# The first two weight chunks piece by piece over both halves of x, in a two-block fp32 decoder kernel

## What is computed

```python
def rmsnorm(x, g):
    xf = x.astype(jnp.float32)
    y = xf * lax.rsqrt(jnp.mean(xf * xf, axis=-1, keepdims=True) + NORM_EPS)
    return (y * g.astype(jnp.float32)).astype(x.dtype)

def split_proj(h, w_in, n_kv):
    proj = h @ w_in          # (256 x 1024) @ (1024 x 2304)
    ...
```

## Time and profile before

| | us |
|---|---|
| median of 3 runs (873.58 to 873.85) | 873.74 |
| the profiled execution | 873.88 |
| its span, first to last instruction | 872.1 |
| TensorE matmuls busy | 861.9 (99%) |
| VectorE busy | 562.4 (64%) |
| ScalarE busy | 509.8 (58%) |
| GpSimd busy | 121.9 (14%) |

### The profile page before, as it was taken

One profiled execution on the slowest core, in us unless ns is written; L12 is line 12 of the kernel. 1 busy time (PEld: TensorE's weight loads), 2 busy tenths in 40 slices (PEclk: granted clock), 3 DMA queues, 4 the chain that ended last, 5 costly groups with the idle time before them and its releaser, 6 DMA issues.

```text
span 872.1 us, 12071 instructions
## 1 busy us (share of the span) xinstructions
PE 861.9 (99%) x4426; PEld 702.8 (81%) x4426; DVE 562.4 (64%) x991; ACT 509.8 (58%) x907; POOL 121.9 (14%) x99
## 2 busy tenths in 40 slices
PE   8999999999999999999999999999999999999996
PEld 5877888778888878888888888888878888888885
DVE  6966866677766777755555446576778655555444
ACT  6668466765886864644444334777865644444332
POOL 0122053110153500000000000153510000000000
PEclk9999999999999999999999999999999999999999
DMA  8823563445533336655555555444345655555531
GB/s 307 281 65 105 187 201 135 147 145 173 175 129 131 129 114 209 209 182 179 187 193 194 193 192 172 151 140 145 99 144 187 211 184 192 193 191 175 194 117 48
DMA packets 94765, 146.15 MB, mean 168 GB/s; under 512 B 6516, under 2 KB 54900, under 8 KB 94708
## 3 DMA queue, kind: packets, MB, share of 16 engines
q1 hardware_dynamic: 92820, 139.52, 48.0%
q0 software_dynamic: 1296, 4.72, 1.5%
q10 hardware_dynamic: 592, 1.15, 0.4%
HBM read 144.32 MB, written 1.05 MB: 167 GB/s over the span
## 4 chain that ended last, share of the span: by engine, by line
PE 93%; DVE 2%; ACT 2%; issue 1%; DMA 1%; SPq 0%; POOLq 0%; POOL 0%; ACTq 0%; DVEq 0%
PE bank L1166 79%; PE bank L1114 7%; PE bank L1317 1%; PE bank L1243 1%; PE bank L1221 1%; PE bank L1218 1%; ACT hyb_E L1559 1%; DMA raw<-in_w_in_a 1%; PE bank L1246 1%; ACT hi L1337 0%; PE bank L1323 0%; DVE hyb_xs L1997 0%; DVE hyb_xs L1989 0%; DVE hyb_xs L1995 0%; DVE hyb_rot L1992 0%
## 5 line engine op out<-in xcount | busy, mean ns | idle before, releaser
L1013 DVE TENSOR_TENSOR lo<-raw,hi 128x1024 fp32r<-128x1024 f32 (+1 forms) x244 | 299.4, 1256 | 101.1 <-ACT hi L1337 98.5
L1337 ACT ACTIVATE hi<-raw 128x1024 fp32r<-128x1024 f32 (+1 forms) x260 | 266.9, 1059 | 109.3 <-PE bank L1166 101.0
L1166 PE MATMUL bank<-hi,xT_hi 128*128 128x512 f32 (+2 forms) x736 | 290.3, 394 | 0.4 <-DVE lo L1667 0.2
L1166 PE MATMUL bank<-hi,xT_lo 128*128 128x512 f32 (+2 forms) x736 | 282.6, 384 | 0.0
L1166 PE MATMUL bank<-lo,xT_hi 128*128 128x512 f32 (+2 forms) x736 | 281.8, 383 | 0.0
L1166 PEld LDWEIGHTS bank<-hi,xT_hi 128*128 128x128 f32 x736 | 138.3, 188 | 30.8 <-issue 4.8
L1166 PEld LDWEIGHTS bank<-hi,xT_lo 128*128 128x128 f32 x736 | 138.2, 188 | 28.2
L1166 PEld LDWEIGHTS bank<-lo,xT_hi 128*128 128x128 f32 x736 | 138.6, 188 | 25.2 <-issue 0.5
L1166 PE MATMUL bank<-hi,hT 128*128 128x512 f32 x352 | 109.6, 390 | 0.0
L1166 PEld LDWEIGHTS bank<-hi,hT 128*128 128x128 f32 x352 | 66.1, 188 | 13.7
L1166 PE MATMUL bank<-lo,hT 128*128 128x512 f32 x176 | 68.5, 389 | 0.0
(11 more groups left out here) (251 smaller groups left out, 941.8 us busy)
## 6 DMA issues: line engine op xcount, KB each, us to landing
raw<-in_w_in SPq DMA_DIRECT2D x26, 1024.0 KB, 5.0
raw<-in_w_gate SPq DMA_DIRECT2D x44, 512.0 KB, 3.7
raw<-in_w_up SPq DMA_DIRECT2D x44, 512.0 KB, 4.7
raw<-in_w_down SPq DMA_DIRECT2D x22, 1024.0 KB, 4.8
raw<-in_w_out SPq DMA_DIRECT2D x20, 1024.0 KB, 5.0
raw<-in_w_in_b SPq DMA_DIRECT2D x10, 1024.0 KB, 5.0
raw<-in_w_in_a SPq DMA_DIRECT2D x7, 1024.0 KB, 7.8
raw<-in_w_in_a SPq DMA_DIRECT2D x4, 256.0 KB, 5.4
```

The costliest lines, as they stand in the source:

```text
L1013: return engine.tensor_tensor(lo[r][:, cols], raw[c.i % RAW][:, cols], hi[r][:, cols].bitcast(F32), ALU.subtract)
L1166: last = nc.tensor.matmul(bank[:, 0:wd], still[a], mv[r][:, off:off + wd], start=c.first and i == 0 and j == 0, stop=c.last and i == len(t ...
L1337: nc.scalar.activation(hi[c.i % SPLIT][:, cols], raw[c.i % RAW][:, cols], ACT.Copy)\
```

## The change

Part by part:

1. **Half-sized transposes.** `first_turn` (four transposes, one bank) becomes `x_rows` (two transposes, one bank); q = 0 or 1 tells which two of the four k. All four `x_rows` of n = 0 stand together on TensorE, after the gains; the four of n = 1 stand together where the eight transposes stood, but the matmuls ahead of them are others (see 3).
2. **The gain is applied while x is rounded.** `first_x` is gone. `x_split` on ScalarE is two ACTIVATEs of 128 columns that read PSUM with the gain column as scale; on VectorE two scalar_tensor_tensor instructions of 128 columns compute PSUM times gain minus hi. Both engines alternate `x_split` with `piece`.
3. **Pieces with both halves of x.** Chunks 0 and 1 are both loaded by eight DMAs of 256 KB and split by eight pieces, and TensorE takes k after k, for each k m = 0 and m = 1. Before the transposes of n = 1 stand k = 0, 1 and 2 (18 matmuls), after them k = 3, then chunk 1.
4. **Queues.** ScalarE's queue issues the identity (`cst`, 64 KB), the gains (4 KB) and x's second rows (256 KB); SyncE's queue issues x's first rows and then all weights.
5. **Warm matmuls.** 7 at the start, none between, 1 at `begin`, on a tile of 128 x 1 that is read with a stride of nought, and whose memset comes first on VectorE.

The core of the diff:

```diff
+    rows = {(m, q): x_rows(sc, 0, m, q) for m in range(M) for q in range(2)}
+    for q in range(2):
+        for m in range(M):
+            x_split(sc, rows[m, q])
+            sc.step("piece")
     sc.step("begin")
 
     def second():
-        first = [first_turn(sc, 1, m) for m in range(M)]
-        sc.step("second_weights")
-        first_split(sc, first[0])
-        sc.step("second_weights")
-        first_split(sc, first[1])
+        rows = {(m, q): x_rows(sc, 1, m, q) for m in range(M) for q in range(2)}
+        for q in range(2):
+            for m in range(M):
+                x_split(sc, rows[m, q])
+            for _ in range(2):
+                sc.step("piece")
         squares(sc, 0)
...
+            if s.kind in ("chunk", "rest") and s.i < 2:
+
+                c, half = (s, 0) if s.kind == "chunk" else (s.of, 1)
+                for k in ((0, 1, 2), (3,))[half] if c.i == 0 else ((0, 1), (2, 3))[half]:
+                    if k % 2 == 0:
+                        pe.wait_ge(piece_lo, (4 * c.i + k) // 2 + 1)
+                    else:
+                        split_done(pe, c.i, k // 2)
+                    for b, wd, ts, m in c.outs:
+                        ended(pe, sc.split_x[c.i, m, k // 2], "vector")
...
         pe.wait_ge(warm_up, 1)
-        warmed(6)
+        warmed(7)
...
             if s.kind == "begin":
-                warmed(3)
+                warmed(1)
...
+        act.dma_start(cst[:, 0:P], t["cst"][:, 0:P]).then_inc(const_in, 16)
         act.dma_start(gain_rows8[:, :], t["norm_g"][0].rearrange("(k p) -> k p", p=P)).then_inc(columns_in, 16)
+        act.dma_start(h[:, 1, 0:512], t["x"][0][P:S, 0:512]).then_inc(x_first[1], 16)
...
+            elif s.kind == "x_split":
+                if s.i == 0:
+                    act.wait_ge(sem["columns", "vector"], 1)
+                ended(act, s.of, "tensor")
+                for i in range(2):
+                    k = 4 * s.n + 2 * s.q + i
+                    last = nc.scalar.activation(xT[0][:, k, s.m * P:(s.m + 1) * P],
+                                                psum[4 + s.bank.at][:, i * P:(i + 1) * P], ACT.Copy,
+                                                scale=gain_cols[:, k:k + 1])
+                done(last, s)
...
+            elif s.kind == "x_split":
                 if s.i == 0:
                     dve.wait_ge(sem["columns", "vector"], 1)
...
+                    last = stt(b, psum[4 + s.bank.at][:, i * P:(i + 1) * P], gain_cols[:, k:k + 1],
+                               a.bitcast(F32), ALU.mult, ALU.subtract)
```

More of the change, by code:

```diff
@@ L1031, in build @@
     for c in chunks:
-        total[c.i % RAW] += 16 * len(c.loads)
+        total[c.i % RAW] += 16 * len(c.loads) if c.i >= 2 else 0
         arrived[c.i] = total[c.i % RAW]
@@ L1055, in load @@
                 off = 0
-                if c.i == 0:
+                if c.i < 2:
                     _, (wt, c0, cw, ks) = c.loads[0]
[L1059 to L1071, removed]
+                    for n, k in enumerate(ks):
+                        sp.dma_start(slot[:, n * cw:(n + 1) * cw], wt[:, k, c0:c0 + cw])\
+                          .then_inc(piece_in[k], 16)
                     return
@@ L1118, in warmed @@
             for _ in range(n):
-                nc.tensor.matmul(psum[3][:, :], warm[:, 0:P], warm[:, :], start=True, stop=True)
+                nc.tensor.matmul(psum[3][:, :], spread(warm[:, :], [P, P]), spread(warm[:, :], [P, 512]),
+                                 start=True, stop=True)
         pe.wait_ge(warm_up, 1)
-        warmed(6)
+        warmed(7)
         for s in sc.steps:
@@ L1128, in _ @@
                   .then_inc(sem["columns", "tensor"], 1)
-            if s.kind == "first_turn":
+            if s.kind == "x_rows":
                 pe.wait_ge(x_in if s.n else x_first[s.m], 16)
                 bank = freed(pe, s.bank)
-                for i in range(4):
-                    c0 = s.n * 512 + i * P
+                for i in range(2):
+                    c0 = s.n * 512 + (2 * s.q + i) * P
                     last = transpose(bank[:, i * P:(i + 1) * P], h[:, s.m, c0:c0 + P])
-                last.then_inc(sem["first_turn", "tensor"], 1)
-                if s.i == 0:
-                    warmed(3)
+                last.then_inc(sem["x_rows", "tensor"], 1)
             if s.kind == "begin":
-                warmed(3)
+                warmed(1)
[8 more added lines that the diff above has]
+                        ended(pe, sc.split_x[c.i, m, k // 2], "vector")
+                        _, kt, off = ts[k]
+                        still = [x[:, kt, m * P:(m + 1) * P] for x in xT]
+                        for j, (a, mv) in enumerate(((0, hi), (0, lo), (1, hi))):
+                            last = nc.tensor.matmul(
+                                psum[2 * b["pair"] + m][:, 0:wd], still[a], mv[c.i][:, off:off + wd],
+                                start=c.first and k == 0 and j == 0, stop=c.last and k == 3 and j == 2)
+                        if c.last and k == 3 and m == 0:
+                            last.then_inc(part_done, 1)
+                if half:
+                    last.then_inc(sem["chunk", "tensor"], 1)
+                continue
             if s.kind in ("chunk", "rest"):
@@ L1143, in _ @@
                     ended(pe, x, "vector")
-                if half == 0 and c.i:
+                if half == 0:
                     split_done(pe, c.i, 0)
@@ L1328, in split @@
         def split(c, half):
-            if c.i == 1 and half == 0:
-                act.wait_ge(second_in, 16)
-            elif half == 0 or c.i == 1:
+            if half == 0:
                 act.wait_ge(raw_in[c.i % RAW], arrived[c.i])
@@ L1365, in _ @@
         for s in sc.steps:
-            if s.kind in ("second_weights", "chunk", "rest"):
+            if s.kind in ("chunk", "rest"):
                 if s.kind == "rest" and s.i == 0:
@@ L1738, in tables @@
             chained(ts(small[:, :, 1, :], small[:, :, 1, :], -1.0, None, ALU.mult))
+        nc.vector.memset(warm[:, :], 1.0).then_inc(warm_up, 1)
         nc.vector.memset(ones[:, :], 1.0)
-        nc.vector.memset(warm[:, :], 1.0).then_inc(warm_up, 1)
         later = []
         for s in sc.steps:
-            if s.kind in ("second_weights", "chunk", "rest"):
+            if s.kind in ("chunk", "rest"):
                 if s.kind == "chunk" and s.i == 4:
```

92 lines of the change are left out of this document (33 added, 59 removed).

## The result

| | before | changed |
|---|---|---|
| median, us (7 runs each, side by side) | 873.91 | 876.89 |
| lowest to highest | 873.58 to 874.81 | 875.95 to 877.64 |
| the profiled execution | 873.88 | 876.69 |
| its span | 872.1 | 874.9 |

The ratio is 1.0033, with a 95% interval of 1.0023 to 1.0043: slower, by 3.0 us where 1.6 were forecast. That is outside the forecast case and just beyond the upper end of the range, 876.8. (Counted from the kernel before as it was measured each time, it is 2.98 us against 3.06, just inside.)

What follows compares the result with a forecast made beforehand. The prediction took TensorE to bound the kernel, with least slack, 0.26 us, in chunk 2. A 1.6 us later thirteenth matmul there gave 873.88 + 1.6 = 875.5, the median 0.14 lower: 875.3 us, range 874.0 to 876.8.

Steps and rivals of the forecast that it cites:

- the forecast case: The main outcome: 875.0 to 875.7 us, around a forecast of 875.3, chance 0.50.
- The slack of 0.26 us in the middle of chunk 2: Before the change, VectorE's `lo` ends at 22.54, and chunk 2's thirteenth matmul, the first needing it, starts at 22.80.
- Table load, first product: At the beginning: tables load behind the first transposes of x, at 5.05; the first product starts at 8.3 against 8.20.
- These come no later than before: The first two transposes of x, for which the table load waits: the first at 4.25 against 4.48.
- either bound: Costs considered for each of VectorE's two scalar_tensor_tensors of 128 columns: 0.32 or 0.48 us, with 0.35 taken.
- ScalarE to the first square, and the chain: ScalarE's work for n = 1 takes 4.24 us; from first square to the end of chunk 2's `lo`, 7.08.
- TensorE up to the transposes of n = 1: 18 matmuls after the first product's start take 4.3 us, putting these transposes at 12.6 against 12.09.
- the sum: 873.88 + 1.6 = 875.5, less 0.14 for the median: 875.3 us.
- Rival B: TensorE's clock comes late, so the first products are 0.43 instead of 0.23 apart: 876.3 to 877.1 us, chance 0.17.
- Rival A: TensorE alone sets the pace, no stall in chunk 2, which starts at 20.2: 872.6 us, chance 0.07.
- C: Part of the loss is absent (earlier x rows, quicker short instructions or tables loaded early): 874.0 to 874.9 us, chance 0.13.
- D: The short instructions at the beginning cost more, first product at 8.6: 875.5 to 876.3 us, chance 0.13.

Runs made afterwards that it cites:

- Experiment 2: The changed kernel with a one-column ACTIVATE ahead of ScalarE's first wait for x, so the tables load early: 875.86 us, ratio 1.0019.
- experiment 1: The changed kernel with four more warm matmuls after x's first rows and three more at the step before the first product: 875.32 us, ratio 1.0018.
- experiment 8: The changed kernel with four warm matmuls after the first transposes, tables loaded early, squares moved into ScalarE's gaps, norm's factor moved later: 872.87 us, ratio 0.9989.
- experiment 6: The changed kernel with x's second rows back on SyncE's queue, behind the first piece: 878.00 us, ratio 1.004; its profiled execution took 875.83.
- experiment 3: The changed kernel with all four squares moved ahead of the splits for n = 1: 875.06 us, ratio 1.0012.
- experiment 5: The changed kernel with chunk 0 cut after k = 1, so 12 matmuls instead of 18 precede the transposes of n = 1: 875.51 us, ratio 1.0019.
- the repeat in 6: The changed kernel with x's second rows back on SyncE's queue, run once more: 878.07 us, ratio 1.0046.
- experiment 4: The changed kernel with added warm matmuls, tables loaded early and all four squares ahead of the splits for n = 1: 874.14 us, ratio 1.0002.
- the second kernel in 6: The changed kernel with x's second rows back on SyncE's queue and four warm matmuls after the first two transpose groups and at begin: 875.72 us, ratio 1.002.
- experiment 7: The kernel before with only the changed kernel's plan of warm matmuls (seven at the start, none between, one at begin): 874.08 us, ratio 1.0000.

## Why the prediction was half right

*What bounds the kernel, and where the loss would show.* Right. The slack of 0.26 us in the middle of chunk 2 was the place, the wait there on VectorE's `lo` is the 1.6 us one, and nothing after 30 us adds to the loss.

*Table load, first product.* Right in mechanism, 0.2 us short in size: the load stands at 5.21 (5.05 forecast). "These come no later than before" was wrong: the first transposes started at 4.67, not at 4.25 and not before 4.48, since TensorE waited 0.40 us for the gains, which ScalarE's queue now issues behind the identity. They then ran faster than before, which gave most of it back. VectorE's pair takes 0.61 us with 0.52 from its start to the subtraction's, less than either bound allowed for two of them one after the other, and the first product is at 8.50, inside 8.3 to 8.6. Experiment 2 shows that the load's place costs 0.7 us in the trace and some 1.0 in the median.

*ScalarE to the first square, and the chain.* Right: 4.10 against 4.24 and 7.14 against 7.08. For the short ACTIVATEs the row of before held: four start 1.02 before the next form does, 0.255 each. The 0.29 of the Trainium skill (ScalarE: Activation LUTs, What ACT_TABLE_LOAD costs) would have made it longer than it was; the measurement decides.

*TensorE up to the transposes of n = 1.* **This is the step that failed.** "Now there are 18, 0.228 apart, and 0.2 for the slow first one" took the high clock for granted: they took 5.67 us instead of 4.3, and from 12.6 the transposes went to 14.17. Of these 1.6 us, 1.4 is pace and 0.2 the later first product. With the warm matmuls of experiment 1 the step holds (4.26 us; the transposes at 12.88, since the first product came at 8.62), and so does the sum (875.32 against 875.3). That the sum agrees to so little is luck: its thirteenth matmul of chunk 2 came 0.2 late (24.58 against 24.4), and about as much was given back later in the span.

*Rival B* named this, and priced it nearly right (876.3 to 877.1; it came to 876.89), but I gave it 0.17 for a wrong reason. "Seven warm matmuls in one stretch are more than the six before" is true and did what it should: the clock was up at about 4.7. I asked when the clock would rise, and not whether it would stay. The pauses that the change makes, 1.49 and 0.80 us on either side of five short operations, were in my own working ("a pause until x's second rows come"), and it fell after them. Before, the warm matmuls between had filled most of these. (The same working says "four busy microseconds to 4.05"; from 1.05 they are three.) The Trainium skill (TensorE: Matmul & The Clock Gate, Part 4: PE-mode transpose) says that transposes don't count as activity as matmuls do. The runs agree in part. With eight transposes, the gains and one warm matmul between 4.1 and 8.5 the clock fell; in experiment 8, with four warm matmuls more, it was up at 4.77 (four transposes in 0.66 us) and the first product at 7.34 still ran at the high pace. But in the fast execution of experiment 6 TensorE had done the same work, with a longer pause ahead of the product, and the clock came up. These runs can't tell a transpose that doesn't count from plain idleness, and no run here shows why one execution goes the one way and another the other. What they do show: five traces of the new order with its few warm matmuls have the clock up for the first four transposes (0.66 or 0.67 us: the changed kernel, experiments 2, 3 and 5, and the repeat in 6), and in all five it is low for the first products; in all four traces with added warm matmuls (experiments 1, 4 and 8, and the second kernel in 6) the products run at the high pace.

*Rival A* fell as the change stands, but once its obstacles are taken away its sum is nearly there: it put chunk 2 at 20.2 and the time at 872.6; experiment 8 has 20.59 and 872.87. That experiment also moved the norm's factor and the squares, so it isn't the change that was forecast.

*Rivals C and D.* C: x's second rows came at 6.8 and the tables weren't loaded ahead; nothing of it happened. D: 0.2 us of it did, in the first product.

## What to carry to other kernels

In a kernel that one engine fills, look up where its smallest slack to the others lies, and ask of a change at the beginning which engine reaches that place last; it may be one that is idle most of the time, and work that it could do in its idle gaps (here the squares) should stand in them. Work that seems useless, such as matmuls on a tile of ones, may be what keeps the clock up over the pauses: whoever moves pauses must move the fillers too. Losses that stand one behind the other ahead of the same wait add up, and pauses ahead of it take a loss up, so the same few warm matmuls cost 1.4 us in one order and nothing in another.

## What the runs showed of the hardware

- The clock of TensorE, once up (four transposes in 0.67 us at 4.67), fell back to 0.50 between 8 and 9 us, and rose between the products at 11.23 and 11.63 in the changed kernel; in the profiled execution of experiment 5, after nearly the same beginning, it was still low at 13.31. One and the same kernel had its products at the high pace in one execution (experiment 6, 875.83 us) and at the low one in another (878.1 us): 2.2 us between executions. The transposes of n = 1 stand 2.27 apart in the two traces (12.93 and 15.20), although the first product of the faster one starts later (8.69 against 8.28): the pace of the products is what differs.
- The column of the granted clock reads 1.00 in windows before the first change of clock that the trace records: in experiment 7 the products up to 10.56 run 0.43 apart, the low pace, under a clock of 1.00. The distance between starts is the safer evidence at a program's beginning.
- In the changed kernel the DMA engines moved 366 GB/s in the fourth microsecond and 383 in the fifth, where they had moved 239 and 168 before. It isn't the queue of x's second rows: with these back on SyncE's (experiment 6) it was 389 and 377, and 375 and 354 in the repeat. Of what else changed in the order of the loads no run tells which did it. On ScalarE's queue x's second rows landed 5.0 us after their issue (5.1 before), behind the first piece on SyncE's 3.7 to 4.2 us.
- ScalarE's load of its tables stands right ahead of the first ACTIVATE, behind whatever that one's place in the queue makes it wait for; one column of useless work ahead of the wait moved it from 5.21 to 2.19.
